# Other orders of walking the moving tokens in the feed-forward matmuls of a two-block network

## The reference

```python
h = rmsnorm(x, norm_ffn[i])
gt, up = jnp.split(h @ w_ffn_in[i], 2, axis=-1)       # 1024 -> 2 x 2816
x = x + (jax.nn.silu(gt) * up) @ w_ffn_out[i]         # 2816 -> 1024
```

## Time and profile before

| | us |
|---|---|
| median of the two runs | 2149.53 |
| lowest, highest | 2149.07, 2149.98 |
| span of the profiled execution | 2148.6 |
| TensorE (PE) busy | 2126.1 (99%) |
| its weight loads (PEld) | 2069.0 (96%) |
| VectorE (DVE) busy | 1640.3 (76%) |
| ScalarE (ACT) busy | 1212.5 (56%) |
| mean DMA rate over the span | 175 GB/s |

### The profile page before, as it was taken

The page is one execution under the profiler, slowest core; times in us unless marked ns, Lnnn a source line. Parts: engine busy times, 40 slices in busy tenths (PEclk is TensorE's granted clock), DMA queues, the critical chain, the costliest instruction groups (busy, mean ns, idle before and its releaser), DMA issues.

```text
span 2148.6 us, 47945 instructions
## 1 busy us (share of the span) xinstructions
PE 2126.1 (99%) x18740; PEld 2069.0 (96%) x18740; DVE 1640.3 (76%) x2626; ACT 1212.5 (56%) x1823; POOL 56.4 (3%) x54
## 2 busy tenths in 40 slices
PE   9999999999999999999999999999999999999998
PEld 8999999999999999899999999999899999999998
DVE  8997877987778766778947877766678947877764
ACT  6646544556656445446658845445446658845443
POOL 0000000000000000000002200000000002200000
PEclk9999999999999999999999999999999999999999
DMA  7434655644456556554544466556554544465553
GB/s 250 158 129 149 207 187 185 201 160 150 138 167 216 185 195 208 171 169 145 177 157 152 149 199 207 187 188 214 172 167 147 177 157 150 149 200 186 187 189 128
DMA packets 102977, 376.54 MB, mean 175 GB/s; under 512 B 11681, under 2 KB 11809, under 8 KB 102305
## 3 DMA queue, kind: packets, MB, share of 16 engines
q1 hardware_dynamic: 101664, 368.66, 52.1%
q10 hardware_dynamic: 1152, 5.58, 0.7%
HBM read 373.14 MB, written 1.05 MB: 174 GB/s over the span
## 4 chain that ended last, share of the span: by engine, by line
PE 90%; DVE 6%; ACT 2%; issue 1%; DMA 0%; DVEq 0%; ACTq 0%
PE acc L772 25%; PE acc L774 24%; PE acc L773 24%; DVE w_lo L1806 2%; PE acc L891 1%; PE acc L892 1%; PE acc L893 1%; PE acc L837 1%; PE acc L836 1%; PE acc L838 1%; ACT w_hi L1325 1%; PE mid L1128 1%; PE mid L1227 1%; DVE pr L2565 0%; PE mid L959 0%
## 5 line engine op out<-in xcount | busy, mean ns | idle before, releaser
L1806 DVE TENSOR_TENSOR w_lo<-w_raw,w_hi 128x1024 fp32r<-128x1024 f32 x694 | 848.0, 1226 | 317.0 <-ACT w_hi L1325 308.7
L1325 ACT CAST w_hi<-w_raw 128x1024 fp32r<-128x1024 f32 x694 | 724.1, 1047 | 537.9 <-PE acc L774 473.1
L772 PE MATMUL acc<-h_hi,w_hi 128*128 128x256 f32 x2096 | 597.2, 285 | 0.3 <-DVE w_lo L1806 0.3
L774 PE MATMUL acc<-h_hi,w_lo 128*128 128x256 f32 x2096 | 586.0, 280 | 0.0
L773 PE MATMUL acc<-h_lo,w_hi 128*128 128x256 f32 x2096 | 585.0, 279 | 0.4 <-issue 0.4
L772 PE MATMUL acc<-g_hi,w_hi 128*128 128x256 f32 x1456 | 409.3, 281 | 0.8 <-DVE w_lo L1806 0.7
L774 PE MATMUL acc<-g_hi,w_lo 128*128 128x256 f32 x1456 | 406.6, 279 | 0.0
L773 PE MATMUL acc<-g_lo,w_hi 128*128 128x256 f32 x1456 | 406.1, 279 | 0.0
L772 PEld LDWEIGHTS acc<-h_hi,w_hi 128*128 128x128 f32 x2096 | 394.7, 188 | 6.6 <-issue 4.9
L773 PEld LDWEIGHTS acc<-h_lo,w_hi 128*128 128x128 f32 x2096 | 394.1, 188 | 1.1 <-issue 0.6
L774 PEld LDWEIGHTS acc<-h_hi,w_lo 128*128 128x128 f32 x2096 | 394.5, 188 | 0.0
(11 more groups left out here) (443 smaller groups left out, 3455.6 us busy)
## 6 DMA issues: line engine op xcount, KB each, us to landing
w_raw<-weights_d SPq DMA_DIRECT2D x695, 512.0 KB, 3.5
p<-p_d ACTq DMA_DIRECT2D x3, 1080.0 KB, 8.5
rdec<-decay_d ACTq DMA_DIRECT2D x2, 768.0 KB, 5.1
p<-p_d SPq DMA_DIRECT2D x1, 1024.0 KB, 10.5
out_d<-work SPq DMA_DIRECT2D x4, 256.0 KB, 2.3
x_all<-x_d SPq DMA_DIRECT2D x1, 516.0 KB, 4.3
w_raw<-weights_d SPq DMA_DIRECT2D x2, 256.0 KB, 5.7
x_all<-x_d SPq DMA_DIRECT2D x1, 512.0 KB, 6.1
```

Of the source, the lines that this page charges most:

```text
L772: mm(dst, wh, hi[:, k, :], start=first and j == 0, stop=False)
L774: done = mm(dst, wl, hi[:, k, :], start=False, stop=last and j == len(ks) - 1)
L1325: nc.scalar.copy(w_hi[:, slot, :], w_raw[:, slot, :]).then_inc(hi_done, 1)
L1806: tt(w_lo[:, slot, :], w_raw[:, slot, :], w_hi[:, slot, :].bitcast(F32), SUB).then_inc(lo_v, 1)
```

## The change

A table `WALKS` gives each of the four feed-forward parts (by `split`) an order for its in stage and one for its out stage. A pair (h, e) cuts the 256 tokens into h equal parts and takes e tokens of each by turns; both the moving operand and the sums in the bank are walked so, and each token's sum stays where it was. "pairs" walks the moving operand over the even tokens and then over the odd ones, and writes the bank in order, so that the bank holds even tokens in its first 128 columns and odd ones in the rest; VectorE's residual addition reads it back crosswise. None leaves the order as it was. So:

| part (`split`) | in stage | out stage |
|---|---|---|
| 0 | chunks of 16 from two halves | chunks of 2 from two halves |
| 1 | chunks of 32 from two halves | every second token |
| 2 | chunks of 8 from two halves | chunks of 64 from two halves |
| 3 | chunks of 16 from four quarters | as before |

The first slab of each in stage (`slab_raw`) and the mixers keep their order. The diff:

```diff
--- before.py
+++ after.py
@@ -38,6 +38,9 @@
 VCOLS = 512
 WARM = 5
 DIRECT = 2
+
+
+WALKS = ((2, 16), (2, 2)), ((2, 32), "pairs"), ((2, 8), (2, 64)), ((4, 16), None)
 
 
 HEADS, KV_HEADS, HD = 8, 2, 64
@@ -760,18 +763,27 @@
 
                 pe.wait_ge(out[t % 4], at.four + (t // 4 + 2))
 
-            def products(at, i, dst, col, width, ks, hi, lo, first=True, last=True, need=None):
-
-
-                slot = i % RING
+            def walked(ap, order):
+
+                if order is None:
+                    return ap
+                if order == "pairs":
+                    return ap.rearrange("p (a b) -> p b a", b=2)
+                return ap.rearrange("p (h c e) -> p c h e", h=order[0], e=order[1])
+
+            def products(at, i, dst, col, width, ks, hi, lo, first=True, last=True, need=None, order=None):
+
+
+                slot, dst = i % RING, dst if order == "pairs" else walked(dst, order)
                 for j, k in enumerate(ks):
                     if need is not None:
                         need(k)
                     a = j * width + col
                     wh, wl = w_hi[:, slot, a:a + P], w_lo[:, slot, a:a + P]
-                    mm(dst, wh, hi[:, k, :], start=first and j == 0, stop=False)
-                    mm(dst, wh, lo[:, k, :], start=False, stop=False)
-                    done = mm(dst, wl, hi[:, k, :], start=False, stop=last and j == len(ks) - 1)
+                    h, l = walked(hi[:, k, :], order), walked(lo[:, k, :], order)
+                    mm(dst, wh, h, start=first and j == 0, stop=False)
+                    mm(dst, wh, l, start=False, stop=False)
+                    done = mm(dst, wl, h, start=False, stop=last and j == len(ks) - 1)
                 return done
 
             def slab_normed(at, i, t):
@@ -817,11 +829,11 @@
                     last = mm(dst, w_hi[:, slot, k * P:k * P + P], g_lo[:, k, :], start=False, stop=k == KD - 1)
                 last.then_inc(used, 1)
 
-            def slab_k8(at, i, t, need=None, hi=h_hi, lo=h_lo):
+            def slab_k8(at, i, t, need=None, hi=h_hi, lo=h_lo, order=None):
 
                 weights_of(at, i)
                 bank(at, t)
-                products(at, i, acc[t % 4][:, 0:T], 0, P, range(KD), hi, lo, need=need).then_inc(used, 1)
+                products(at, i, acc[t % 4][:, 0:T], 0, P, range(KD), hi, lo, need=need, order=order).then_inc(used, 1)
 
             def part_k4(at, i, t, ks, hi, lo, need=None):
 
@@ -861,7 +873,7 @@
                         if ks[-1] == KD - 1:
                             done.then_inc(used, 1)
 
-            def slabs_long(at, i, t, n, blocks, hi, lo, need=None):
+            def slabs_long(at, i, t, n, blocks, hi, lo, need=None, order=None):
 
                 bank(at, t)
                 for m in range(n):
@@ -869,7 +881,7 @@
                         last_mean(0)
                     weights_of(at, i + m)
                     ks = range(m * KD, min(m * KD + KD, blocks))
-                    products(at, i + m, acc[t % 4][:, 0:T], 0, P, ks, hi, lo, m == 0, m == n - 1, need).then_inc(used, 1)
+                    products(at, i + m, acc[t % 4][:, 0:T], 0, P, ks, hi, lo, m == 0, m == n - 1, need, order).then_inc(used, 1)
 
             def slab_rows(at, i):
 
@@ -895,22 +907,23 @@
 
             def ffn(at, second):
                 si, ti, so, to = ffn_layout(second)
+                order_in, order_out = WALKS[at.split]
                 slab_raw(at, si, ti, gain_hi, gain_lo)
                 for j in range(1, 4):
-                    slab_k8(at, si + j, ti + j, None, g_hi, g_lo)
+                    slab_k8(at, si + j, ti + j, None, g_hi, g_lo, order_in)
                     if j == 1:
                         mean(at, 1)
                 with pe.Fori(1, FF // 2) as it:
                     now = Later(at, it, 4, 4)
                     for j in range(4):
-                        slab_k8(now, si + j, ti + j, None, g_hi, g_lo)
+                        slab_k8(now, si + j, ti + j, None, g_hi, g_lo, order_in)
 
                 def act_ready(k):
 
                     pe.wait_ge(ff_lo, at.ffn + (k + 1))
 
                 for n in range(KD):
-                    slabs_long(at, so + 3 * n, to + n, 3, FF, f_hi, f_lo, act_ready if n == 0 else None)
+                    slabs_long(at, so + 3 * n, to + n, 3, FF, f_hi, f_lo, act_ready if n == 0 else None, order_out)
 
             def s5_turned(at, g):
 
@@ -1974,7 +1987,10 @@
                     if early:
                         residual(at, n - 1)
                     wait_used(dve, at, so + 3 * n + 2)
-                    tt(x[:, n, :], x[:, n, :], acc[(to + n) % 4][:, 0:T], ADD).then_inc(out[(to + n) % 4], 1)
+                    part, mine = acc[(to + n) % 4][:, 0:T], x[:, n, :]
+                    if WALKS[at.split][1] == "pairs":
+                        part, mine = part.rearrange("p (b a) -> p a b", b=2), mine.rearrange("p (a b) -> p a b", b=2)
+                    tt(mine, mine, part, ADD).then_inc(out[(to + n) % 4], 1)
                     if n and not early:
                         residual(at, n - 1)
                 residual(at, KD - 1)
```

## The result

The changed kernel takes 2248.07 us (2247.35 to 2248.78), 98.5 us more than the 2149.53 before: a ratio of 1.046, 95% interval 1.0445 to 1.0479. Slower was forecast, 2268.7 us in a range of 2148 to 2285. The sum is 20.6 us off, and its terms are further off than that: the first out stage cost 34.4 us less than forecast, and the stages forecast at nothing cost 12.9 us, so two errors cancel in part.

The account below looks back on a forecast made before the run. TensorE was taken to bound the kernel, busy 99% of the span. Added costs 59.5 + 59.5 + 0.2 = 119.2 us; 2148.6 + 0.9 + 119.2 = 2268.7 us, range 2148 to about 2285.

Parts of the forecast that it names:

- the prediction's own signs: First two out stages at 121 us each if right; wrong if a stage with chunks of 8 and more grows over 2 us.
- What bounds: TensorE, busy 99% of the span; in the feed-forward matmuls the moving columns bind at 0.440 ns each, not the weight load.
- Part 3: Second out stage, every second token read: each group of four words serves two columns, 59.5 us more, bounds 0 and 62.9.
- Part 2: First out stage, chunks of 2 from two halves: each access serves two columns, 59.5 us more, bounds 0 and 62.9.
- Part 1: Four in stages and third out stage, chunks of 8 to 64: whole groups of four words, cost 0, at most 59.6 us.
- Part 4: VectorE's eight residual additions in the second out stage: jumping reads cost 0.2 us each, one on the chain, so +0.2 us.
- Part 5: What follows slower stages: weight splits wait longer and the DMA ring empties more slowly, but nothing else becomes late or gains.
- A: Rival, all walked stages: TensorE fetches ahead and two words a fetch suffice, so no change, 2149.7 us; chance 0.33.
- rival D: All broken walks at half pace, chunked stages too: 643.7 us more, 2793 us; chance 0.03.
- B: Rival: TensorE pays 0.78 ns at each break in a run, a step of two being none: 2262.0 us; chance 0.08.
- C: Rival, first two out stages: one of the two fine walks slow, the other free, 2209.2 us; chance 0.07.
- E: Rival, walked stages: alternating halves eases the stream, at best 10.7 ns a matmul, 61 us faster, 2088 us; chance 0.04.

Follow-up runs that it names:

- v1: Kernel before, with feed-forward activations laid even tokens in a tile's first half, odd in its second, and read by turns from the halves: 2090.15 us, ratio 0.9722.
- v2: v1 with the second network's tiles r, s and m laid down and read by turns too: 2080.33 us, ratio 0.9676 to the kernel before.
- e1: Changed kernel with walks of one side only: chunks of 16 took 126.6 us read-only, 121.5 write-only (in stages); every fourth token read, 123.1 us (out stage).
- e7: Changed kernel with reads in chunks of 2 by turns from two runs 544 to 4096 bytes apart: in stages 173.9 to 174.7 us, out 88.1 to 89.0.
- e8: Changed kernel with reads in chunks of 2 from two runs 0 to 512 bytes apart: in stages busy 171.5 us at 256 and 128 bytes, 115.8 at 16.
- e4: Changed kernel with reads of single tokens by turns: from two places 111.7 to 112.5 ns a matmul, four 140.0, eight 222.2, 16 places 219.9.
- e5: Changed kernel with other reads: turns 8 bytes apart 62.5 us (out); from halves with a step of 2, 121.5 us (in); one token throughout, 115.6 us (in).
- e6: Changed kernel with other walks: each token read twice 111.9 ns a matmul, chunks of 2 from 16 parts 220.0, chunks of 4 from 32 parts 117.8.

## Why the prediction was right in sign, and where it was off

**The total (partly luck).** 2248.07 lies in the range of 2148 to 2285, but that range was wide enough for the rival of no change; the narrower 2255 to 2280 for the forecast's own case missed by 7 us. By the prediction's own signs it was wrong in two places: the first out stage was to take 121 us and took 87.6, and no stage with chunks of 8 and more was to grow by over 2 us, where three grew by 5.0, 2.4 and 5.1.

**What bounds (right).** Each ns of a matmul's start distance was paid: 99.2 us in the windows, 98.5 in the median. That the columns bind and not the weight load, and that the 0.440 ns a column is above the engine's own pace and "belongs to the stream itself", was right and more useful than I saw: the 5.6 ns between 117.5 and the floor of 111.9 hang on the order of the read alone, and can be had (v1, v2).

**Part 3, every second token (right in size).** 59.5 us forecast, 61.2 measured, at 233.1 ns a matmul. The reasoning had one reader whose access serves two columns. Theory 3 has two readers, each with a new access for every one of its 128 columns. The product 128 × 1.77 ns is the same, so a wrong picture could give the right number; that was luck. Every fourth token refuted the one reader: 233.1 ns (e1), where it would have taken 458.

**Part 2, chunks of 2 (mis-sized).** 59.5 us forecast, 25.1 measured. The step that failed is "every two columns lie elsewhere, so each access serves two": it counts an access of 1.76 ns for every two columns, and takes no account of how many places are read by turns. With two places a matmul costs 165.9 ns, 47.5 more than before and not 112.7, at any distance from 32 bytes to 4 KB (e7, e8). With four places and more the price is 220.0 to 232.5 ns, about what was forecast for this one. Theory 3c, by which a stream still has the words of the place before its last, is the picture for it, and is inferred. The write is free, as said.

**Part 1, the coarse walks (cost 0 forecast, 12.9 us measured).** Its upper bound of 59.6 held. The step that failed is "Each chunk holds whole groups of four words", hence "Cost 0". Chunks of 16 and 8 from halves cost 4.8 and 4.9 ns more a matmul, chunks of 32 2.3, chunks of 16 from quarters 0.4, chunks of 64 nothing. It is the read that costs this (e1). No theory here gives these few ns: the number of breaks doesn't (16 breaks cost 4.8 or 0.4), nor does theory 3, by which they all go as in order. Smaller and larger misses of the same kind are chunks of 8 from quarters (129.0 ns), of 4 from halves (128.4), and of 8 from eight parts, which go below the price in order (115.8). The cause stays open.

**Part 4, the additions.** 0.2 us each forecast, 0.008 measured. The row taken for it jumps in its write to SBUF; here a read of PSUM jumps. The row was of the wrong side; whether it is the reading or the PSUM that makes the jump cheap, no run sets apart.

**Part 5 (right).** Nothing else became late: TensorE's busy time grew by 95.8 us and the span by 97.0, and VectorE's busy time is the same to 2.2 us.

**The rivals.** A, and with it the rule that two words of an access suffice, is refuted for TensorE: every second token uses two of four and takes twice as long. The size of the access in that rule of the Trainium skill ("Advanced Engine Details and Errata", Memory Cachelines), 16 bytes, agrees with e4 and e5: turns 16 bytes apart run at the floor, turns 8 bytes apart don't. The other sentence of that section, behind rival D, that any non-contiguous pattern on PSUM slows matmuls significantly, isn't borne out for chunks of two words and more: writes in chunks of 2 took 61.9 us like writes in order. B, near the forecast in total, falls with the stages: it had a step of two at no cost and the third in stage 25.8 us longer, where these measured 61.2 and 5.1 us. C had one fine walk free; neither was. E, to which I gave 0.04, was right in its thought and wrong in its place: turns do free the stream, by 5.6 ns of the 10.7 that I allowed, but single columns by turns, which the change doesn't have.

What is shown: that the read pays and the write doesn't, the prices of some fifty walks, and that the distance of two places doesn't matter for chunks of 2 from 32 bytes to 4 KB. That words are read in fours, by two streams that take the even and the odd columns, is inferred; it is the one picture found that fits the factor of two and the floor, and it foretold the first two stages of e6. Not tried: other widths of word, other column counts than 256, and walks whose period is odd, which would test the parity directly.

## What to carry to other kernels

Ask of a walk over a matmul's moving operand, in fp32r with 256 columns, how many of the even columns in a row, and of the odd, lie in one group of four words: four is the floor (112 ns), two about as in order (115.8 to 133.7 ns measured, 117.5 in order itself), one is nearly twice as long (219 to 233 ns). Three walks fall outside this count: chunks of 2 from only two places (166 ns from 32 bytes apart on, 112 ns at 16 bytes) and single words from four (140 ns). If TensorE is the bound, lay the data so that single columns come by turns from two halves; it costs its writers a step of two. Writes of sums in chunks of two words were free here, and a jumping read of PSUM by VectorE cost 8 ns in 414.

## What the runs showed of the hardware that was not expected

- Reading single columns by turns from two places 16 to 512 bytes apart is 4.8% faster than in order: 111.9 against 117.5 ns, the same as reading one token 256 times.
- A step of 2, 4 or 8 words costs nearly the same: 233.1, 233.1 and 218.6 ns.
- Chunks of 2 words cost 165.9 ns from two places and 225.5 from four; single words from four places by turns cost 140.0, from eight 222.2.
- VectorE pays for a jumping write to SBUF (620 against 421 ns) and next to nothing for a jumping read of PSUM (422 against 414 ns).
- Chunks of 8 from eight parts are cheaper than in order (115.8 ns), from quarters dearer (129.0); why is open.
- After an added wait of 3.2 us the granted clock was 0.67 over the next 4.9 us (e8), with starts 0.21 us apart at first, where they are 0.165 apart at full clock.
